# Second FFN up-projection, rounds 3 to 11: seven half-token products in place of eight block products

## The chip, the cores and the metric

The kernel runs on one core of a Trainium2 chip. The metric is the device time of one execution in microseconds. Everything, weights included, is float32; the inputs lie in DRAM.

## The reference, cut to what matters

Two transformer blocks run one after the other over 512 tokens of width 1024. The change touches only the up-projection of the second block's feed-forward part and what hangs on it:

```
h = rms_norm_2(x, ffn_norm_g[l]) * (1 + scale_f) + shift_f
u, v = jnp.split(h @ w_up[l], 2, axis=-1)          # w_up: 1024 x 5632
u = causal_depthwise_conv(u, conv_w[l], conv_b[l])  # width 3 over the tokens
x = x + gate_f * ((jax.nn.silu(u) * v) @ w_down[l])
return rms_norm_2(x, final_g)
```

## The kernel before, in words

**Layout.** Features lie on the 128 partitions, tokens on the free axis: `h` is eight slices of 128 features by 512 tokens. A *tile* `s` is 128 output features. Tiles 156 to 199 (`S_UP2` to `S_DOWN2`) are the second up-projection, tiles 200 to 223 the down-projection behind it. A tile is eight slices `k` deep.

**Float32 by three products.** Every operand is split in a high part (rounded to the matmul's format) and a low part (the rest). `split_product` (L2281 to L2285) issues three matmuls for each slice: high weight by high `h` (L2283), high weight by low `h` (L2284), low weight by high `h` (L2285). A full tile is 8 x 3 = 24 matmuls of 512 columns. Before it, ScalarE (ACT) writes `w_hi` from the landed weights `raw` (L1251 in this stage, L920 elsewhere), and GpSimd (POOL) writes `w_lo = raw - w_hi` (function `lo`, L814 to L821; the instruction has line L820). There are four `w_hi`/`w_lo` buffers and two `raw` buffers; a `raw` buffer holds the two tiles of a *unit*. `w_hi` of tile s waits for tile s-4 to be done, a load waits for the `w_lo` of the tiles that held its buffer.

**A round** is four tiles: two tiles of `u` (t = 0, 1) and the two tiles of `v` for the same features. 11 rounds cover 2816 features. For each t, ACT takes `u` out of PSUM with the middle tap and the bias (L1258), VectorE (DVE) adds the two other taps of the convolution (L1936, L1939), ACT applies silu (L1262), DVE multiplies with the `v` tile out of PSUM (L1930), ACT writes `g_hi` (L1265) and DVE `g_lo = product - g_hi` (L1955). The product stands in `uv`. Each engine walks this list in its own program order, as loops (`ffn_act`, `ffn_dve`, `ffn_pe`); the order between engines is by semaphores alone. `freed["dve"]` counts tiles whose PSUM bank DVE has released: TensorE (PE) waits for it before it starts a tile in the same bank (tile s in bank s % 4 here).

**Ahead of it** the first round is run in halves of 256 tokens because `h` arrives in pieces (`half_tile`, `two_halves`; their matmuls also have the lines L2283 to L2285); DVE and ACT work there on the norm. `xT` holds the residual and is next needed by the down-projection (`last_residual`, L2208).

Of the kernel before, what the change touches and what calls it, by code (L numbers as in the profile page):

```python
# [37 lines left out]
LEVELS = [1, 2, 4, 8, 16, 32, 64]  # L38

# [47 lines left out]
def value_of_step(u):  # L87

    s = step_tile(u - 1)
    return VALUE_TILES.index(s) if u and u % 2 == 0 and s in VALUE_TILES else None  # L90

# [67 lines left out]
def build(nc, a, out):  # L159
# [5 lines left out]
    with ctx:  # L165
# [118 lines left out]
        uv = hn  # L284
        assert max(top1, ada_at + 9216) <= end
# [30 lines left out]
        ps = [nc.alloc_psum_tensor(f"ps{i}", [P, 512], F32) for i in range(8)]  # L316
# [59 lines left out]
        values_turned, values_copied = sem("values_turned"), sem("values_copied")  # L376
        act_chain, dve_chain, pool_chain = sem("act_chain"), sem("dve_chain"), sem("pool_chain")
# [32 lines left out]
        for n in range(S_END // 2):  # L410
# [69 lines left out]
        HALF = T // 2  # L480
# [231 lines left out]
        def _(sp):  # L712
# [85 lines left out]
        def _(pool):  # L798
# [15 lines left out]
            def lo(s, slot=None, count=None):  # L814

                pool.wait_ge(hi_done, s + 1 if count is None else count)
# [3 lines left out]
                pool.tensor_tensor(w_lo[slot % 4][:, 0:nk, :], part[:, :, slot % 2 * P:(slot % 2 + 1) * P],  # L820
                                   w_hi[slot % 4][:, 0:nk, :].bitcast(F32), ALU.subtract).then_inc(lo_done, 1)  # L821
# [77 lines left out]
        def _(act):  # L899
# [7 lines left out]
            def hi(s):  # L907
# [8 lines left out]
                if s >= 4:  # L916
# [3 lines left out]
                act.activation(w_hi[s % 4][:, 0:nk, :], part[:, :, s % 2 * P:(s % 2 + 1) * P],  # L920
# [516 lines left out]
            ffn_act(S_UP2, 1)  # L1437
# [38 lines left out]
        def _(dve):  # L1476
# [742 lines left out]
            ffn_dve(S_UP2, 1)  # L2219
# [60 lines left out]
        def _(pe):  # L2280
# [6 lines left out]
            def tile(s, x, xl, k0=0, first=True, last=True, part=(0, None), ready=None, signal=True):  # L2287
# [567 lines left out]
            ffn_pe(S_UP2, 2)  # L2855
            for n in range(22):
# [5 lines left out]
                down_part(S_DOWN2, n, parts(g_lo_done, FT + 4) if n in (0, 2, 4) else None)  # L2862

            def last_half(q, at=None, between=None):
# [3 lines left out]
                if half == 0:  # L2868
                    pe.wait_ge(lo_done, s + 1)
# [61 lines left out]
```

## Time and profile before

| | |
|---|---|
| median of 3 runs | 1354.01 us (1353.15 to 1357.63) |
| profiled execution: span of its one core | 1350.1 us |
| what lies around the span: median less span | 3.9 us |
| PE busy | 1333.5 us, 99% |
| TensorE clock granted, mean | 0.999 |
| the 36 tiles that change, first matmul to first matmul of tile 200 | 1024.00 to 1219.84 us |

The profiled execution is listed by its span; no time of its own beside it was shown, so the difference to the median stands for what lies around it. Times in rows are microseconds from the start of the span. A matmul's duration in a row contains its way through the array; the rate of a stream is read from the distance between starts.

### The profile page before, as it was taken

How to read it: one execution, taken by the hardware profiler on the slowest of the kernel's cores; microseconds unless marked ns; L12 is line 12 of the kernel's file. 1: busy time of each engine (PE TensorE's matmuls, PEld its weight loads, DVE VectorE, ACT ScalarE, POOL GpSimd, SP SyncE). 2: the span in 40 equal slices, each digit the busy share in tenths (PEclk: the TensorE clock that was granted, in tenths of full speed). 3: DMA queues.
4: the chain of work that ended last, by engine and by line, in shares of the span. 5: the costliest groups of instructions: out<-in, count | busy, mean ns of one | idle time of the engine just before them, and what ended most of it. 6: DMA issues, size and time to landing. Idle time of an engine off the chain costs nothing.

```text
span 1350.1 us, 21809 instructions
## 1 busy us (share of the span) xinstructions
PE 1333.5 (99%) x8014; PEld 1125.5 (83%) x8014; DVE 802.3 (59%) x1626; ACT 618.4 (46%) x1064; POOL 619.3 (46%) x334
## 2 busy tenths in 40 slices
PE   8999999999999999999999998999999999999998
PEld 7878888888998888888889976788998888888887
DVE  5898875456778676767897968714652323221222
ACT  7237566464354545453223535675453434432222
POOL 7545232126364444444544479623354444444441
PEclk9999999999999999999999999999999999999999
DMA  7931121115535444445663232122132222233221
GB/s 218 228 99 47 49 63 49 32 35 171 169 109 160 150 152 146 145 130 164 210 196 122 78 94 65 33 63 63 64 124 93 93 93 93 94 99 104 86 86 63
DMA packets 188315, 146.22 MB, mean 108 GB/s; under 512 B 21561, under 2 KB 186659, under 8 KB 188240
## 3 DMA queue, kind: packets, MB, share of 16 engines
q1 hardware_dynamic: 186528, 144.59, 34.9%
q8 instruction: 50, 0.82, 0.3%
q10 hardware_dynamic: 1200, 0.36, 0.1%
q0 software_dynamic: 512, 0.25, 0.1%
q14 instruction: 25, 0.20, 0.0%
HBM read 143.08 MB, written 2.10 MB: 108 GB/s over the span
## 4 chain that ended last, share of the span: by engine, by line
PE 91%; POOL 4%; DVE 2%; issue 1%; ACT 1%; DMA 0%; DVEq 0%; POOLq 0%; ACTq 0%
PE ps L2283 27%; PE ps L2285 27%; PE ps L2284 27%; POOL w_lo L820 2%; PE ps L2477 2%; PE ps L2533 1%; PE ps L2562 1%; POOL hg L656 1%; PE ps L2762 1%; DVE qd L2077 1%; DVE hf L2085 1%; POOL kd_odd L652 0%; PE ps L2735 0%; PE ps L2367 0%; PE ps L2806 0%
## 5 line engine op out<-in xcount | busy, mean ns | idle before, releaser
L820 POOL TENSOR_TENSOR w_lo<-raw,w_hi 128x1024 fp32r<-128x1024 f32 (+2 forms) x224 | 518.5, 2318 | 666.5 <-ACT w_hi L920 401.6
L2283 PE MATMUL ps<-h_hi,w_hi 128*128 128x512 f32 (+1 forms) x1336 | 497.2, 372 | 0.0
L2284 PE MATMUL ps<-h_lo,w_hi 128*128 128x512 f32 (+1 forms) x1336 | 493.3, 369 | 0.0
L2285 PE MATMUL ps<-h_hi,w_lo 128*128 128x512 f32 (+1 forms) x1336 | 493.0, 369 | 0.0
L2283 PEld LDWEIGHTS ps<-h_hi,w_hi 128*128 128x128 f32 x1336 | 251.8, 188 | 46.0 <-issue 4.7
L2285 PEld LDWEIGHTS ps<-h_hi,w_lo 128*128 128x128 f32 x1336 | 251.8, 188 | 42.8
L2284 PEld LDWEIGHTS ps<-h_lo,w_hi 128*128 128x128 f32 x1336 | 251.9, 189 | 40.7
L920 ACT ACTIVATE w_hi<-raw 128x1024 fp32r<-128x1024 f32 (+2 forms) x136 | 133.5, 984 | 215.3 <-PE ps L2285 194.5
L1251 ACT ACTIVATE w_hi<-raw 128x1024 fp32r<-128x1024 f32 x88 | 93.3, 1060 | 211.8 <-PE ps L2285 211.8
L2283 PE MATMUL ps<-g_hi,w_hi 128*128 128x512 f32 (+1 forms) x394 | 144.9, 368 | 0.0
L2285 PE MATMUL ps<-g_hi,w_lo 128*128 128x512 f32 (+1 forms) x394 | 144.4, 366 | 0.0
L2284 PE MATMUL ps<-g_lo,w_hi 128*128 128x512 f32 (+1 forms) x394 | 144.3, 366 | 0.0
L1887 DVE SCALAR_TENSOR_TENSOR ps<-ada,cond,ps 128x128 f32<-128x128 f32 x336 | 119.6, 356 | 12.0
L2283 PEld LDWEIGHTS ps<-g_hi,w_hi 128*128 128x128 f32 x394 | 74.3, 189 | 12.2
L2284 PEld LDWEIGHTS ps<-g_lo,w_hi 128*128 128x128 f32 x394 | 74.3, 189 | 12.1
L2285 PEld LDWEIGHTS ps<-g_hi,w_lo 128*128 128x128 f32 x394 | 74.3, 189 | 12.0
L1936 DVE SCALAR_TENSOR_TENSOR sq<-ps,small,sq 128x511 f32<-128x511 f32 x44 | 33.0, 750 | 78.1 <-ACT sq L1258 74.8
L2208 DVE SCALAR_TENSOR_TENSOR xT<-ps,small,xT 128x256 f32<-128x256 f32 (+1 forms) x22 | 13.3, 604 | 106.1 <-PE ps L2285 106.1
L1655 DVE SCALAR_TENSOR_TENSOR ps<-z,small,ps 128x512 f32<-128x512 f32 x106 | 70.4, 754 | 0.0
L1930 DVE TENSOR_TENSOR hn<-ps,sq 128x512 f32<-128x512 f32 x22 | 15.2, 691 | 85.9 <-ACT sq L1262 85.9
L1122 ACT ACTIVATE sc<-sc,stat 128x128 f32<-128x128 f32 (+3 forms) x64 | 35.5, 557 | 26.7 <-DVE stat L1668 26.5
L1806 DVE COPY pT<-ps 128x128 f32<-128x128 f32 (+3 forms) x32 | 15.7, 490 | 48.1 <-PE ps L2533 27.0
(373 smaller groups left out, 1703.1 us busy)
## 6 DMA issues: line engine op xcount, KB each, us to landing
ada<-in_ada_w SPq DMA_DIRECT2D x48, 512.0 KB, 3.8
raw<-in_ffn_w_up SPq DMA_DIRECT2D x22, 1024.0 KB, 4.9
raw<-in_w_up SPq DMA_DIRECT2D x22, 1024.0 KB, 4.9
raw<-in_w_in SPq DMA_DIRECT2D x21, 1024.0 KB, 5.1
raw<-in_ffn_w_down SPq DMA_DIRECT2D x8, 896.0 KB, 5.9
raw<-in_w_down SPq DMA_DIRECT2D x8, 896.0 KB, 4.6
raw<-in_w_in SPq DMA_DIRECT2D x16, 256.0 KB, 3.7
raw<-in_w_out SPq DMA_DIRECT2D x4, 1024.0 KB, 5.2
```

The source lines that it names most:

```text
L820: pool.tensor_tensor(w_lo[slot % 4][:, 0:nk, :], part[:, :, slot % 2 * P:(slot % 2 + 1) * P], w_hi[slot % 4][:, 0:nk, :].bitcast(F32), ALU ...
L920: act.activation(w_hi[s % 4][:, 0:nk, :], part[:, :, s % 2 * P:(s % 2 + 1) * P], ACT.Copy).then_inc(hi_done, 1)
L1122: act.activation(x, x, ACT.Exp, scale=-1.0, bias=stat[:, 2 * (j % 2) + g:2 * (j % 2) + g + 1], accum_out=stat[:, 4 + 2 * (j % 2) + g:5 + 2 ...
L1251: act.activation(w_hi[s % 4][:, :, :], part[:, :, s % 2 * P:(s % 2 + 1) * P], ACT.Copy).then_inc(hi_done, 1)
L1655: ins = dve.scalar_tensor_tensor(out=out, in0=src, scalar=w, in1=was, op0=ALU.mult, op1=ALU.add)
L1806: dve.tensor_copy(pT[:, m % 2, 1, 0:L2], ps[7][:, 0:L2]).then_inc(pw_copied, 1)
L1887: dve.scalar_tensor_tensor(out=acc, in0=src, scalar=c, in1=acc, op0=ALU.mult, op1=ALU.add).then_inc(ada_scaled, 1)
L1936: dve.scalar_tensor_tensor(out=u[:, t, 1:T], in0=src[:, 0:T - 1], scalar=col(wname, m + wide), in1=u[:, t, 1:T], op0=ALU.mult, op1=ALU.add ...
L2283: pe.matmul(out_ap, w, x, start=first, stop=False, **kw)
L2284: pe.matmul(out_ap, w, xl, start=False, stop=False, **kw)
L2285: return pe.matmul(out_ap, wl, x, start=False, stop=last, **kw)
L2477: ins = pe.matmul(ps[4 + g][:, 0:L], queries[i][g][part][:, t * P:(t + 1) * P], keys[b][g][:, 0:L], start=part == 0, stop=part == 1)
```

## The change

Rounds 1 and 2 (counted from 1) stay plain tiles, unrolled. The other nine rounds, 36 tiles, become 18 *pairs* p = 0 to 17. A pair is what was one unit: 256 output features by 512 tokens, 1024 deep. It is taken as a two-by-two block product: weight blocks of 512 deep by 128 features, `h` blocks of 512 deep by 256 tokens. Seven products of sums of blocks, each 4 slices deep, 3 matmuls to a slice, 256 columns wide (12 matmuls), take the place of eight. Pairs with even p are `u` tiles, with odd p the `v` tiles of the same round.

- **Sums of `h`** once: T1 to T4, 128 x 1024 elements each. DVE: three adds for T1, two for T2, two for T4 (`t_add`); POOL: three for T3 (`third_sum`). ACT writes their high parts (`t_part_hi`), DVE their low parts (`t_part_lo`). Their room is that of `xT`, so `xT` is stored to DRAM (`x_kept`, 2 MB, two DMAs) and loaded back at the end of the stage. T4 goes over the second-token-half of `h`'s first four slices, after the last plain tile.
- **Sums of weights**, per pair: four adds or subtracts of 128 x 512 by DVE, `w_add(p, 5)`, `(p, 7)`, `(p, 6)`, `(p, 3)`; both operands in SBUF, partly in place in `raw`. Each of the seven products then needs its own `w_hi` (ACT, 128 x 512) and `w_lo` (POOL, 128 x 512): `product_hi`, `product_lo`. The four buffers are used as eight halves.
- **PSUM.** Four banks to a pair. Product 1 gives a value that ACT copies (`copy_one`) as the seed of another region; product 5 is copied to SBUF (`copy_five`); DVE writes two sums in PSUM (`seed_c12`, `make_c22`) on which later products go on adding.
- **Order.** `PRODUCTS` lists the products: 1, 5 of pair 0, then for each p: 6, 2, [1 of p+1], 7, 3, [5 of p+1], 4. PE, ACT and POOL follow it. `g_prod` is a new buffer for the products of `u` and `v`.
- **Loads.** A pair's unit comes as two DMAs of 512 KB; the second waits for the `w_lo` of product 4 of pair p-2, the first for its four sums and the `w_lo` of product 7.

The core of the diff:

```diff
+PLAIN = 2
+PAIR_TILE = S_UP2 + 4 * PLAIN
+NPAIR = (S_DOWN2 - PAIR_TILE) // 2
+PRODUCTS = [(0, 1), (0, 5)]
+for _p in range(NPAIR):
+    PRODUCTS += [(_p, 6), (_p, 2)] + [(_p + 1, 1)] * (_p + 1 < NPAIR) + [(_p, 7), (_p, 3)] \
+        + [(_p + 1, 5)] * (_p + 1 < NPAIR) + [(_p, 4)]
...
@@ SyncE
+                if p < 2:
+                    sp.wait_ge(lo_done, splits(2 * n - 3))
+                else:
+                    sp.wait_ge(w_summed, ONCE + 4 * (p - 2) + 4)
+                    sp.wait_ge(lo_done, product_splits(p - 2, 7))
+                dst, src = k_half(a["w_up_2"][0], (m % 2) * FFN + (m // 2) * 256, n, 0)
+                sp.dma_start(dst, src).then_inc(raw_top[n % 2], 16)
+                unit(n)
...
@@ GpSimd
+            for s in range(S_UP2 + 4, PAIR_TILE):
+                lo(s)
+            third_sum()
+            for p, j in PRODUCTS:
+                product_lo(p, j)
...
@@ ScalarE, product_hi(q)
+                if q < 8:
+                    act.wait_ge(tile_done, PAIR_TILE - 3 + q // 2)
+                else:
+                    after_product(act, *PRODUCTS[q - 8])
...
@@ VectorE
+            def w_add(p, j):
+                if j == 5:
+                    dve.wait_ge(raw_top[u % 2], LANDED + 16 * (p // 2 + 1))
+                    dve.wait_ge(raw_in[u % 2], RAW_COUNT[u])
...
+                    ins = dve.tensor_tensor(w_of(p, 5), w_block(p, 1, 0), w_block(p, 1, 1), ALU.add)
...
+                else:
+                    dve.wait_ge(w_summed, ONCE + 4 * p + 3)
+                    dve.wait_ge(lo_done, product_splits(p, 2))
+                    ins = dve.tensor_tensor(w_of(p, 3), w_block(p, 0, 1), w_of(p, 6), ALU.subtract)
...
+            for r in range(PLAIN - 1):
+                for t in range(2):
+                    taps2(r, t)
+                if r == PLAIN - 2:
+                    t_add(0, hi_of(B12), hi_of(B11), ALU.subtract)
+                    t_add(0, t_sum[0], lo_of(B12), ALU.add)
+                    t_add(0, t_sum[0], lo_of(B11), ALU.subtract, True)
+                for t in range(2):
+                    gated_up(r, t)
...
+            t_add(1, hi_of(B22), t_sum[0], ALU.subtract)
+            t_add(1, t_sum[1], lo_of(B22), ALU.add, True)
+            t_part_lo(0)
+            g_low(r - 1, 0)
+            g_low(r - 1, 1)
+            taps2(r, 0)
+            w_add(0, 5)
+            dve.wait_ge(t_summed, ONCE + 2)
+            taps2(r, 1)
+            w_add(0, 7)
+            w_add(0, 6)
+            gated_up(r, 0)
+            w_add(0, 3)
+            w_add(1, 5)
+            w_add(1, 7)
+            gated_up(r, 1)
+            t_add(3, hi_of(B21), t_sum[1], ALU.subtract)
+            t_add(3, t_sum[3], lo_of(B21), ALU.add, True)
+            t_part_lo(1)
+            t_part_lo(2)
+            g_low(r, 0)
+            g_low(r, 1)
+            w_add(1, 6)
+            t_part_lo(3)
+            for p in range(NPAIR):
+                r, kind = PLAIN + p // 2, p % 2
+                last = PLAIN + (p - 1) // 2
+                if kind:
+                    taps2(last, 1)
+                elif p:
+                    gated_up(last, 1)
+                seed_c12(p)
+                if p and not kind:
+                    g_low(last, 0)
+                    g_low(last, 1)
+                if p + 1 < NPAIR:
+                    w_add(p + 1, 3)
+                make_c22(p)
+                if p + 2 < NPAIR:
+                    w_add(p + 2, 5)
+                    w_add(p + 2, 7)
+                if kind:
+                    gated_up(r, 0)
+                else:
+                    taps2(r, 0)
+                if p + 2 < NPAIR:
+                    w_add(p + 2, 6)
...
@@ TensorE, product(p, j)
+                pe.wait_ge(lo_done, product_splits(p, j))
+                if j == 1:
+                    pe.wait_ge(freed["dve"], FREED[PAIR_TILE + 2 * (p - 2) if p > 1 else PAIR_TILE - 4][1])
+                elif j == 5:
+                    pe.wait_ge(freed["dve"], FREED[PAIR_TILE + 2 * p - 3 if p > 1 else PAIR_TILE - 1][1])
...
+                elif j == 6:
+                    pe.wait_ge(one_copied, ONCE + p + 1)
+                elif j == 7:
+                    pe.wait_ge(c12_seeded, ONCE + p + 1)
+                elif j == 4:
+                    pe.wait_ge(c22_made, ONCE + p + 1)
+                for k in range(4):
+                    ins = split_product(out, w_hi[w][:, ks.start + k, :], w_lo[w][:, ks.start + k, :], x[:, k, :], xl[:, k, :],
+                                        j in (1, 5) and k == 0, k == 3, skip_group_check=True)
```

For product 5 of pair 0 the wait on `freed["dve"]` is for tile 163, which `gated_up(1, 1)` releases (here r counts from 0).

## Rows read from the trace of the kernel before

**Rows 1.** The page: busy time by engine, and the 40 slices of TensorE and its clock.

```profile
PE 1333.5 (99%) x8014; PEld 1125.5 (83%) x8014; DVE 802.3 (59%) x1626; ACT 618.4 (46%) x1064; POOL 619.3 (46%) x334
...
PEclk9999999999999999999999999999999999999999
```

**Rows 2.** Windows: us; busy (count) of PE, PEld, DVE, ACT, POOL; clock; DMA share; GB/s.

```profile
1002.20:1024.00 21.80, 21.80 (x99) 18.04 (x97) 7.31 (x8) 9.37 (x12) 11.95 (x6) 1.00 0.43 145
1024.00:1219.80 195.80, 195.80 (x865) 162.22 (x864) 56.87 (x72) 84.28 (x108) 86.26 (x36) 1.00 0.29 95
```

**Rows 3.** Timeline of TensorE: 28 starts of 256 columns; first matmuls of tiles 164, 200.

```profile
985.83 0.28 PE L2285 MATMUL ps<-h_hi,w_lo 128*128 128x256 f32 x1
...
989.07 0.28 PE L2285 MATMUL ps<-h_hi,w_lo 128*128 128x256 f32 x1
...
1024.00 0.39 PE L2283 MATMUL ps<-h_hi,w_hi 128*128 128x512 f32 x1
...
1219.84 0.39 PE L2283 MATMUL ps<-g_hi,w_hi 128*128 128x512 f32 x1
```

**Rows 4.** Groups by line and shape, 244 to 312 us: 128x512 parts on POOL and ACT.

```profile
L820 POOL TENSOR_TENSOR w_lo<-raw,w_hi 128x512 fp32r<-128x512 f32 x12 | 17.4, 1447 | 47.5 <-ACT w_hi L920 47.5
L920 ACT ACTIVATE w_hi<-raw 128x512 fp32r<-128x512 f32 x12 | 7.6, 629 | 10.4 <-PE ps L2285 10.2
```

**Rows 5.** Timeline of POOL and DVE, 300 to 312 us: 128x512 parts of both.

```profile
302.93 0.69 DVE L1850 TENSOR_TENSOR cv_lo<-acc,cv_hi 128x512 fp32r<-128x512 f32 x1
...
303.02 1.75 POOL L820 TENSOR_TENSOR w_lo<-raw,w_hi 128x512 fp32r<-128x512 f32 x1 [0.98 <-ACT w_hi L920]
...
311.18 1.30 POOL L820 TENSOR_TENSOR w_lo<-raw,w_hi 128x512 fp32r<-128x512 f32 x1 [0.98 <-ACT w_hi L920]
```

**Rows 6.** Timeline of DVE and POOL, 821 to 829 us: 128x1024 operations of both.

```profile
821.10 1.23 DVE L2085 TENSOR_TENSOR hf<-hf 128x1024 f32<-128x1024 f32 x1 [1.41 <-POOL hg L656]
822.36 3.27 DVE L2077 TENSOR_TENSOR qd<-hq,hf 128x1024 f32<-128x1024 f32 x1
...
821.14 3.40 POOL L820 TENSOR_TENSOR w_lo<-raw,w_hi 128x1024 fp32r<-128x1024 f32 x1
824.50 3.34 POOL L652 TENSOR_TENSOR kd_odd<-hk,hg 128x1024 f32<-128x1024 f32 x1
```

**Rows 7.** Timeline of POOL and DVE about one `g_lo` of the stage, then without POOL.

```profile
1047.09 2.40 POOL L820 TENSOR_TENSOR w_lo<-raw,w_hi 128x1024 fp32r<-128x1024 f32 x1 [3.04 <-ACT w_hi L1251]
...
1048.71 1.34 DVE L1955 TENSOR_TENSOR g_lo<-hn,g_hi 128x512 f32 x1 [0.36 <-ACT g_hi L1265]
...
408.79 1.29 DVE L1955 TENSOR_TENSOR g_lo<-hn,g_hi 128x512 f32 x2 [0.32 <-ACT g_hi L1265]
```

**Rows 8.** Groups by line and shape, 1002 to 1219 us.

```profile
L1258 ACT ACTIVATE sq<-ps,small 128x512 f32<-128x512 f32 x20 | 15.2, 759 | 0.0
...
L1930 DVE TENSOR_TENSOR hn<-ps,sq 128x512 f32<-128x512 f32 x21 | 14.5, 691 | 81.1 <-ACT sq L1262 81.1
```

**Rows 9.** Timeline of POOL and DVE in the first round of the stage.

```profile
997.42 9.52 POOL L820 TENSOR_TENSOR w_lo<-raw,w_hi 128x1024 fp32r<-128x1024 f32 x4 [11.18 <-ACT w_hi L1251]
...
1000.67 0.75 DVE L1939 SCALAR_TENSOR_TENSOR sq<-ps,small,sq 128x510 f32<-128x510 f32 x1
```

**Rows 10.** DMA issues by line: KB each, median us from issue to landing.

```profile
raw<-in_w_conv_br SPq DMA_DIRECT2D x4, 512.0 KB, 3.4
...
out<-y_out SPq DMA_DIRECT2D x7, 256.0 KB, 2.0
```

**Rows 11.** Timeline: taps of one tile beside `w_lo`; a PSUM operation on 256 columns.

```profile
1053.27 0.75 DVE L1936 SCALAR_TENSOR_TENSOR sq<-ps,small,sq 128x511 f32<-128x511 f32 x1 [2.62 <-ACT sq L1258]
1054.17 0.75 DVE L1939 SCALAR_TENSOR_TENSOR sq<-ps,small,sq 128x510 f32<-128x510 f32 x1 [0.15 <-DVE sq L1936]
...
1052.54 2.40 POOL L820 TENSOR_TENSOR w_lo<-raw,w_hi 128x1024 fp32r<-128x1024 f32 x1 [3.04 <-ACT w_hi L1251]
...
990.74 0.49 DVE L1502 SCALAR_TENSOR_TENSOR ps<-xT,small,ps 128x256 f32<-128x256 f32 x1
```

More of the change, by code:

```diff
@@ new lines, in _ @@
+            for r in range(PLAIN - 1):
+                for j in range(4):
+                    hi(up_tile(r + 1, 0, j))
+                    if j < 2:
+                        first_tap(r, j)
+                    else:
+                        silu(r, j - 2)
+                if r < PLAIN - 2:
+                    g_high(r, 0)
+                    g_high(r, 1)
+            r = PLAIN - 1
+            t_part_hi(0)
+            g_high(r - 1, 0)
+            g_high(r - 1, 1)
+            product_hi(0)
@@ new lines, in _ @@
+            first_tap(r, 0)
+            t_part_hi(1)
+            product_hi(1)
+            first_tap(r, 1)
+            silu(r, 0)
+            product_hi(2)
+            product_hi(3)
+            silu(r, 1)
+            product_hi(4)
+            t_part_hi(2)
+            product_hi(5)
+            product_hi(6)
+            copy_one(0)
+            product_hi(7)
+            g_high(r, 0)
+            copy_five(0)
+            product_hi(8)
+            g_high(r, 1)
+            t_part_hi(3)
@@ new lines, in _ @@
+            for p in range(NPAIR):
+                r, kind = PLAIN + p // 2, p % 2
+                last = PLAIN + (p - 1) // 2
+                q0 = PRODUCT[p, 6] + 7
+                if p and not kind:
+                    g_high(last, 0)
+                if kind:
+                    first_tap(last, 1)
+                product_hi(q0)
+                if kind:
+                    silu(last, 0)
+                product_hi(q0 + 1)
+                if kind:
+                    silu(last, 1)
+                elif p:
+                    g_high(last, 1)
+                product_hi(q0 + 2)
+                if p + 1 < NPAIR:
+                    copy_one(p + 1)
+                    product_hi(q0 + 3)
+                    product_hi(q0 + 4)
+                if not kind:
+                    first_tap(r, 0)
+                if p + 1 < NPAIR:
+                    product_hi(q0 + 5)
+                    copy_five(p + 1)
+                    product_hi(q0 + 6)
@@ L1438, in _ @@
+            for s in range(S_DOWN2, S_DOWN2 + 4):
+                hi(s)
+            for t in range(2):
+                g_high(FT // 2 - 1, t)
             for n in range(20):
@@ new lines, in gated_up, with g_low @@
+            def gated_up(r, t):
+                n = 2 * r + t
+                dve.wait_ge(silu_done, FT + n + 1)
+                dve.wait_ge(tile_done, up_tile(r, 1, t) + 1)
+                dve.tensor_tensor(g_prod[:, n, :], up_out(r, 1, t), ua[:, t, :], ALU.mult).then_inc(freed["dve"], 1)
+            def g_low(r, t):
+                n = 2 * r + t
+                dve.wait_ge(g_hi_done, FT + n + 1)
+                dve.tensor_tensor(g_lo[:, n, :], g_prod[:, n, :], g_hi[:, n, :].bitcast(F32), ALU.subtract).then_inc(g_lo_done, 1)
@@ L2221, in scaled_out @@
+            r = FT // 2 - 1
+            gated_up(r, 1)
+            for t in range(2):
+                g_low(r, t)
+            dve.wait_ge(x_back, LANDED + 32)
             def scaled_out(k, cols):
@@ L2611, in ffn_pe @@
                             second_sum(b)
+            def ffn_pe(s0, b):
+                first_round(s0, b)
                 with pe.Fori(0, FT // 2 - 1) as i:
```

257 lines of the change are left out of this document (228 added, 29 removed).

## The prediction, on record before the changed kernel ran

> **What bounds the kernel now.** I read the page first: TensorE is busy 99% of the span at full clock [rows 1]. Then the windows of the stage: in the nine rounds that change PE has no idle time at all, POOL works 86 us of 196, DVE 57, ACT 84 [rows 2]. Then the timeline, for the rate of the stream. The 36 tiles, 864 matmuls of 512 columns, take 1219.84 - 1024.00 = 195.84 us, 0.2267 us each; 27 steps of 256-column matmuls take 3.24 us, 0.120 us each [rows 3]. So only matmuls count, as long as the other engines keep up; the reader should see how much room they have now, because the change spends it. Last I looked at how POOL and DVE behave when both work on SBUF, for both get more of exactly that.
>
> **What the change takes off PE.** 18 pairs x 7 products x 12 = 1512 matmuls of 256 columns: 1512 x 0.120 = 181.4 us. Against 195.8 us that is **-14.4 us** (-7.4%, not 12.5%: a half-width matmul costs 53% of a full one). Two extra 256-column matmuls in tile 163: +0.2.
>
> A page would make this more. The Trainium skill (TensorE: Matmul & The Clock Gate, Back-to-back issue gap) gives a warm gap of N/2.4 ns plus about 2.5 ns, by which halving the width costs almost nothing: 864 x 215.8 ns less 1512 x 109.2 ns would be 21.3 us, an estimate by that page. The rows show 226.7 and 120 ns; they decide.
>
> **What a product costs beside PE.** ACT: 7 parts of 0.63 a pair [rows 4], 4.4 us, two PSUM copies below 0.5 each [rows 11], and per pair one tap, silu and high part of at most 0.76 [rows 8]: under 8 of 10.1 us. ACT has cover. Loads: 1 MB a pair as before. A 512 KB load lands in 3.4 us [rows 10], SBUF-to-DRAM is 2.0 us for 256 KB; the 2 MB of `xT`, issued behind the load that follows `w_lo` of tile 159 (near 987), have until 1011: at most 8 x 2.0 = 16 us, so ready near 1003. Hidden; at the end the load back has 25 us until the first residual. Cost nothing; if the store came at 1013 it would add its 2 us.
>
> **DVE and POOL exclude each other.** `w_lo` of 128x512 takes 1.30 us alone [rows 5]. When a DVE operation with both operands in SBUF runs at its start (302.93 to 303.62), it ends at 304.77, which is 1.15 us after DVE. Longer ones alternate strictly: DVE ends at 822.33, POOL 2.21 us later (824.54), the waiting DVE operation 1.09 us later (825.63), POOL again 2.21 us later (827.84) [rows 6]. In the stage itself `g_lo` waits until `w_lo` ends at 1049.49 and ends 0.56 us later, 1.34 us in all; two of them without POOL take 1.29 together [rows 7]. A DVE operation with one operand in PSUM isn't touched: taps take 0.75 in the middle of a `w_lo` [rows 11], the product `ps,sq` 0.69 [rows 8]. So I count, for 128x512: POOL 1.26 back to back (for 128x1024 four take 9.52, 0.03 less each than alone [rows 9]), 1.15 after DVE; DVE 0.56 after POOL. Each two-operand DVE operation then costs a busy POOL 0.56 + 1.15 - 1.26 = 0.45 us.
>
> **Steady state, per round (two pairs).** POOL: 14 x 1.26 = 17.6. DVE's two-operand operations: 8 `w_add`, 2 `g_low`: 10 x 0.45 = 4.5. Sum **22.1 us**, against PE's 20.2. DVE's own list, laid against a POOL that is never idle: a run of two-operand operations advances 1.71 each, one that follows other work waits for the next end of a `w_lo`. Even pair: gated (0.69), seed (0.42), three of them, `make_c22` (0.42), two, taps (1.65), one, ends near 11.6; odd pair: taps, seed, one, `make_c22`, two, gated, one, ends at 19.7. In the odd pair `make_c22` must also wait for product 7 (some 1 us). So DVE needs near 21, POOL 22.1: both over PE's 20.2. Seeds stay on time or about 2 us late in odd pairs, which is the same loss seen on PE. Loss: (22.1 - 20.2) = 1.9 to 2.1 a round (DVE and POOL waiting on each other in turn), 16 pairs with a full list: **+16 us**. Bound below: `w_add` costs POOL nothing, 17.6 < 20.2, no loss. Above: no `w_lo` overlaps with any wait of DVE's, 17.6 + 10 x 0.68 = 24.4 a round, +34. The value is near the middle because rows 6 show the alternation itself.
>
> **Start of the pairs.** On the old clock PE finishes tile 163 at 1024.0 and would start product 7 of pair 0 (the sixth) at 1024.2 + 5 x 1.44 = 1031.4. DVE's list, in order:
> - taps of round 1 end 1001.4 [rows 9]. The three T1 adds (128x1024) alternate with the `w_lo` that POOL has in hand from 997.42: 1002.2 + 3 x 1.09 + 2 x 2.21 = 1009.9. Two gated products: 1011.2 (tile 162 needs them at 1013.1: just in time).
> - POOL's three T3 operations end at 1012.1, 1015.4, 1018.7; between them the T2 adds; `t_part_lo(0)` 1019.8.
> - `w_lo` of the first product, two `g_low` 1022.1, taps 1023.8, `w_add(0,5)` 1024.4, ACT's part and tap, taps 1027.5, two `w_add`, gated 1029.4.
> - `w_add(0,3)` overwrites a block whose `w_lo` (fourth product) must be done: ACT 0.7 and two `w_lo` after `w_add(0,6)` at 1028.8, so 1032.2; it ends 1032.8. Two more `w_add` at 1.71: 1036.2. `gated_up(1,1)`: **1036.9**. Only this releases the bank that product 5, the second, waits for. PE stands from 1025.7: +11.2.
> - Two T4 adds, each behind a `w_lo`: 1038.5, 1040.8; one more `w_lo` 1041.9, `t_part_lo(1)` 1043.0. Product 6 needs it and could have gone at 1038.5: +4.5.
> - `t_part_lo(2)`, two `g_low`, `w_add(1,6)`, `t_part_lo(3)` with POOL idle, seed: 1047.5; product 7 starts 1047.6: +0.3 to 0.5.
> Sum 1047.6 - 1031.4 = **+16.2 us**. Bound below: gated_up ready at 1024.0 and only the T4 sum behind it (0.7 + 2 x 1.1 + 1.1 = 4.0 after 1024, product 6 was due at 1027.1): +1 to +3. Above: every item one `w_lo` later, +25.
>
> **Sum.** -14.4 + 0.2 + 16.0 + 16.2 = +18.0; the last pairs have no `w_add` left and run at PE's pace, already in the 16 pairs. The down-projection's own `w_hi` and `w_lo` fit: POOL is through before PE's last product. Span 1350.1 + 18.0 = 1368.1; with the 3.9 us that lie around it, as in the median before, **1372.0 us**.
>
> **Rivals.**
> - *No exclusion in this pattern (strided adds slip between), start on time.* Steady loss 0, start +1 to +3: 1354.0 - 14.4 + 2 = **1342**. For it: engine totals of 86 and 57 in 196 us look roomy [rows 2]. Against: rows 5 to 7 without exception. It decides only if a `w_add` under a `w_lo` takes 0.68. Chance 0.10.
> - *Half of it:* either the start or the steady loss fails (say DVE finds POOL idle early, or a lead of eight half buffers carries POOL through). -14.4 + 16 = **1356**, 1350 to 1362. For it: eight halves are 11.5 us of lead, but a stalled start doesn't let it grow beyond eight. Chance 0.18.
> - *Lock waits as summed* (my forecast): 1362 to 1384. Chance 0.57.
> - *Another link closes the ring:* the second half load of pair p+2 waits for the `w_lo` of product 4 of pair p, and DVE stands in order before `w_add(p+2,5)` until it lands. From that add: ACT 0.7, two `w_lo` 3.0, load 3.4 to 4, next add 1.2: 8.3 to 9 a pair, under 11. If loads landed 3 us later it would reach 12 a pair: +16 more, **1388**. Or TensorE's clock falls in the stalls: rows 1 show full clock but no stall like 11 us; at half clock (0.24 us a matmul) the three or four products after each early stall cost +5. Chance of over 1384: 0.15.
> The Trainium skill (TensorE: Matmul & The Clock Gate, HAM oscillation) says that idle gaps put the array at half clock; no row here shows such a gap, so its price is only in this last case.
>
> **How the numbers follow.** The likeliest case gives 1372. Its own range is 1362 to 1384. The range of 8 in 10 leaves out the faster rival and the far end: 1355 to 1385. Within 0.3% (4 us: 1350 to 1358) is about what a measurement of this kernel can't tell from no change. Faster: the first rival and a tail of the second, 0.13. Same: most of the second's lower part, 0.10. Slower: 0.77.
>
> **What the profile after would show.** Right: PE idle for some 10 us near 1026, just before the second product's matmuls, released by DVE's product of round 2; DVE adds of 128x512 at mean near 1.1 to 1.3 us where 0.68 is their own; POOL parts of 128x512 with mean 1.45 to 1.55, no idle time; one round (14 products) in 22 us; 256-column steps of 0.120 inside a product; ACT with idle time. Wrong: a POOL mean of 1.3, rounds of 20.2 us, no PE gap. If rounds take over 23 us with POOL idle and DVE waiting for a DMA, the ring of the load is it. If steps inside a product are over 0.12, it is the clock.

## The result, and the profile after

The changed kernel takes **1379.66 us** (median of 4 runs, 1377.55 to 1384.74), the kernel before 1353.63 in the same comparison: ratio 1.0196, 95% interval 1.017 to 1.0222. So it is 26.0 us slower; 1372.0 (1355 to 1385) was forecast. The profiled execution of after took 1381.54, with a span of 1379.8.

The page of the kernel after, busy time by engine and two slice lines (before: [rows 1]):

```profile
PE 1331.7 (97%) x8664; PEld 1151.4 (83%) x8664; DVE 952.4 (69%) x1745; ACT 650.4 (47%) x1174; POOL 739.8 (54%) x427
...
PE   8999999999999999999999998999986989899998
POOL 7545232135445444445543888424377999995441
PEclk9999999999999999999999999999998999999999
```

PE's busy time has hardly moved, but the span has grown by 29.7 us: PE has slices at 8 and 6 in the last third, and POOL stands at 9 in five slices. Windows of the kernel after (columns as in [rows 2]): the last plain tiles, the start of the pairs, the rest of them.

```profile
1006.42:1028.47 22.05, 22.05 (x101) 18.26 (x100) 21.91 (x13) 5.94 (x8) 18.86 (x7) 1.00 0.30 96
1028.47:1056.00 27.53, 12.84 (x92) 12.20 (x91) 20.94 (x21) 12.40 (x22) 15.87 (x12) 0.81 0.13 39
1056.00:1249.52 193.52, 175.62 (x1424) 171.81 (x1422) 163.30 (x168) 107.62 (x201) 178.11 (x116) 1.00 0.31 95
```

The stage of the 36 tiles lasts 1249.52 - 1028.47 = 221.05 us, against 195.84 [rows 3]: +25.2. The first pair also began 4.5 us later than tile 164 had; 0.3 of that arose about the two added matmuls, the rest before 930 us, in code that isn't changed (a granted clock of 0.97 between 800 and 900 us and of 0.83 between 920 and 930, where the profiled execution of before had 1.00). In the twelve variants below the pairs begin anywhere from 1024.2 to 1028.0, so this differs from one execution to the next. After the stage both kernels need 130.3 us. So what the change costs, it costs in the stage. What TensorE waited for in it (PE's waits, kernel after: us in all, times, longest):

```profile
PE ps L2671 <- DVE ps L2535: 14.5, 10, 1.6
PE ps L2671 <- DVE g_prod L2510: 12.1, 1, 12.1
PE ps L2671 <- DVE ps L2539: 4.5, 8, 0.6
PE ps L2671 <- DVE t_lo L2527: 1.6, 1, 1.6
```

L2535 is `seed_c12`, L2539 `make_c22`, L2510 `gated_up`, L2527 `t_part_lo`. The waits of the start, from PE's timeline (two matmuls of product 5, three steps apart, stand between them):

```profile
1042.14 0.55 PE L2671 MATMUL ps<-t_hi,w_hi 128*128 128x256 f32 x1 [12.09 <-DVE g_prod L2510]
...
1043.56 0.41 PE L2671 MATMUL ps<-t_hi,w_hi 128*128 128x256 f32 x1
...
1044.20 0.41 PE L2671 MATMUL ps<-t_hi,w_hi 128*128 128x256 f32 x1
...
1046.62 0.39 PE L2671 MATMUL ps<-t_hi,w_hi 128*128 128x256 f32 x1 [1.58 <-DVE t_lo L2527]
...
1052.23 0.36 PE L2671 MATMUL ps<-t_hi,w_hi 128*128 128x256 f32 x1 [1.02 <-DVE ps L2535]
```

Product 7 of pair 0 starts 23.76 us into the stage, where five products of 1.44 need 7.2: **16.6 us lost at the start**: 15.3 in the three gaps, and 1.3 in 13 slow steps (a step is the time from one matmul's start to the next, slow from 0.15 us on), 11 of them at half clock. From 1036 to 1044 us the granted clock is 0.50, and there a step takes (1044.20 - 1043.56) / 3 = 0.213 us in place of 0.120. For the rounds, groups by line and shape of POOL (1028 to 1250 us) and DVE (1056 to 1220 us):

```profile
L938 POOL TENSOR_TENSOR w_lo<-raw,w_hi 128x512 fp32r<-128x512 f32 x107 | 161.6, 1541 | 20.6 <-ACT w_hi L1590 20.6
...
L2486 DVE TENSOR_TENSOR raw<-raw 128x512 f32<-128x512 f32 x15 | 25.1, 1674 | 0.5
L2494 DVE TENSOR_TENSOR raw<-raw 128x512 f32<-128x512 f32 x14 | 23.8, 1698 | 20.3 <-POOL w_lo L938 20.3
```

The `w_add` of products 7 and 3 take 1.67 and 1.70 us (0.69 beside a short `w_lo`, run 1 below), and DVE stands 20.3 us more ahead of product 3's (L2494). One round on DVE, and on POOL (timelines, kernel after):

```profile
1096.02 0.42 DVE L2535 TENSOR_TENSOR ps<-ps,rstd 128x256 f32<-128x256 f32 x1
1096.35 2.56 DVE L2515 TENSOR_TENSOR g_lo<-g_prod,g_hi 128x512 fp32r<-128x512 f32 x2
1100.17 1.70 DVE L2494 TENSOR_TENSOR raw<-raw 128x512 f32<-128x512 f32 x1 [1.26 <-POOL w_lo L938]
...
1111.67 1.70 DVE L2494 TENSOR_TENSOR raw<-raw 128x512 f32<-128x512 f32 x1 [1.66 <-POOL w_lo L938]
...
1094.90 9.81 POOL L938 TENSOR_TENSOR w_lo<-raw,w_hi 128x512 fp32r<-128x512 f32 x6
...
1109.03 7.21 POOL L938 TENSOR_TENSOR w_lo<-raw,w_hi 128x512 fp32r<-128x512 f32 x5 [1.35 <-ACT w_hi L1590]
```

Six rounds, from the seed at 1086.61 to that at 1224.45, take 137.84 us, **22.97 each**; 14 products of 1.44 are 20.16. Of the 221.05 us, 23.76 are the start and 174.2 the other 121 products; the other 23.1 are lost in the rounds.

### The profile page after: what moved, and what is told of

It reads as the page before. It is cut to its first block, busy times and chain, and to the rows that moved or that the text cites. A ratio compares the mean times of both kernels' runs of the same rounds, so it can differ in the third digit from the quotient of the medians.

```text
span 1379.8 us, 23168 instructions
## 1 busy us (share of the span) xinstructions
PE 1331.7 (97%) x8664; PEld 1151.4 (83%) x8664; DVE 952.4 (69%) x1745; ACT 650.4 (47%) x1174; POOL 739.8 (54%) x427
## 4 chain that ended last, share of the span: by engine, by line
PE 68%; DVE 13%; POOL 11%; issue 4%; DMA 2%; ACT 1%; DVEq 0%; SPq 0%; ACTq 0%; POOLq 0%
PE ps L2671 20%; PE ps L2672 19%; PE ps L2673 19%; POOL w_lo L938 6%; DVE ps L2140 3%; POOL w_lo L932 2%; DMA ada<-in_ada_w 2%; PE ps L2865 2%; PE ps L2921 1%; PE ps L2950 1%; DVE raw L2490 1%; DVE raw L2486 1%; DVE hn L2483 1%; POOL hg L751 1%; DVE sq L2500 1%
## 5 line engine op out<-in xcount | busy, mean ns | idle before, releaser
L932 POOL TENSOR_TENSOR w_lo<-raw,w_hi 128x1024 fp32r<-128x1024 f32 (+2 forms) x188 | 435.7, 2322 | 546.2 <-ACT w_hi L1053 413.2
L2671 PE MATMUL ps<-h_hi,w_hi 128*128 128x512 f32 (+1 forms) x1336 | 469.4, 351 | 4.5 <-DVE ps L2539 4.5
L2672 PE MATMUL ps<-h_lo,w_hi 128*128 128x512 f32 (+1 forms) x1336 | 464.0, 347 | 0.0
L2673 PE MATMUL ps<-h_hi,w_lo 128*128 128x512 f32 (+1 forms) x1336 | 463.4, 347 | 0.0
L2672 PEld LDWEIGHTS ps<-h_lo,w_hi 128*128 128x128 f32 x1336 | 253.9, 190 | 29.7
L1053 ACT ACTIVATE w_hi<-raw 128x1024 fp32r<-128x1024 f32 (+2 forms) x144 | 141.7, 987 | 219.6 <-PE ps L2673 190.5
L938 POOL TENSOR_TENSOR w_lo<-raw,w_hi 128x512 fp32r<-128x512 f32 x108 | 163.9, 1548 | 20.6 <-ACT w_hi L1590 20.6
L1590 ACT ACTIVATE w_hi<-raw 128x512 fp32r<-128x512 f32 x108 | 66.1, 623 | 74.9 <-DVE raw L2494 44.3
L2671 PE MATMUL ps<-t_hi,w_hi 128*128 128x256 f32 x216 | 62.6, 290 | 28.1 <-DVE ps L2535 14.5
L1384 ACT ACTIVATE w_hi<-raw 128x1024 fp32r<-128x1024 f32 x44 | 46.6, 1058 | 90.4 <-PE ps L2673 90.4
L2672 PEld LDWEIGHTS ps<-g_lo,w_hi 128*128 128x128 f32 x394 | 74.3, 188 | 12.1
L2671 PEld LDWEIGHTS ps<-t_hi,w_hi 128*128 128x128 f32 x216 | 41.9, 194 | 30.3 <-issue 27.3
```

Source lines behind the costliest of these rows:

```text
L932: pool.tensor_tensor(w_lo[w_slot(slot)][:, 0:nk, :], part[:, :, slot % 2 * P:(slot % 2 + 1) * P], w_hi[w_slot(slot)][:, 0:nk, :].bitcast(F ...
L938: pool.tensor_tensor(w_lo[w][:, ks, :], w_of(p, j), w_hi[w][:, ks, :].bitcast(F32), ALU.subtract).then_inc(lo_done, 1)
L1053: act.activation(w_hi[w_slot(s)][:, 0:nk, :], part[:, :, s % 2 * P:(s % 2 + 1) * P], ACT.Copy).then_inc(hi_done, 1)
L1384: act.activation(w_hi[s % 4][:, :, :], part[:, :, s % 2 * P:(s % 2 + 1) * P], ACT.Copy).then_inc(hi_done, 1)
L1590: act.activation(w_hi[w][:, ks, :], w_of(p, j), ACT.Copy).then_inc(hi_done, 1)
L2671: pe.matmul(out_ap, w, x, start=first, stop=False, **kw)
```

## The experiments

"Stage" is the time from the first product's first matmul to the first one of tile 200, in the profiled execution. TensorE's own work there is 181.4 us. The last column is its waiting in us in the stage; a slow step behind a wait isn't in it.

| kernel | time, us | ratio to before, 95% | stage | PE's waits |
|---|---|---|---|---|
| before | 1353.6 | | 195.8 | 0 |
| after | 1379.66 | 1.0196 (1.017 to 1.0222) | 221.1 | 32.7 |
| 1: `w_lo` short | 1350.73 | 0.9977 (0.9967 to 0.9988) | 192.7 | 7.2 |
| 2: `w_add` short | 1354.30 | 1.0005 (0.9993 to 1.0016) | 196.3 | 10.9 |
| 3: gate moved | 1379.82 | 1.0199 (1.0182 to 1.0216) | 220.2 | 30.0 |
| 4: sum 3 in another block | 1370.31 | 1.0125 (1.0108 to 1.0142) | 211.5 | 24.7 |
| 5: as 4, start reordered | 1373.32 | 1.0159 (1.0142 to 1.0176) | 213.0 | 24.4 |
| 6: as 4, one block in PSUM | 1356.07 | 1.0029 (1.0018 to 1.0039) | 197.7 | 12.8 |
| 7: as 4, two blocks in PSUM | 1357.73 | 1.0032 (1.0021 to 1.0042) | 198.9 | 12.8 |
| 8: as 7, start reordered | 1358.40 | 1.0044 (1.0031 to 1.0057) | 199.1 | 12.4 |
| 9: as 7, banks swapped | 1352.16 | 0.9988 (0.9976 to 1.0) | 193.5 | 9.2 |
| 10: as 4, banks swapped | 1365.40 | 1.0079 (1.0062 to 1.0096) | 208.7 | 21.4 |
| 11: as 9, start trimmed | 1353.70 | 0.9997 (0.9982 to 1.0013) | 195.9 | 7.4 |
| 12: as 11, gaps filled | 1352.72 | 0.9998 (0.9986 to 1.001) | 193.4 | 3.7 |

The kernel before ran anew in each comparison, with medians of 1353.2 to 1354.6.

**1 and 2. Take the exclusion away, from either side.**

```diff
-                 pool.tensor_tensor(w_lo[w][:, ks, :], w_of(p, j), w_hi[w][:, ks, :].bitcast(F32), ALU.subtract).then_inc(lo_done, 1)
+                 few = slice(0, 16)
+                 pool.tensor_tensor(w_lo[w][:, ks, few], w_of(p, j)[:, :, few], w_hi[w][:, ks, few].bitcast(F32),
+                                    ALU.subtract).then_inc(lo_done, 1)
```

> Edit to the changed kernel: each of POOL's 126 w_lo operations of the pairs works on 16 of the 128 columns of its part (64 elements in place of 512), so most of the low parts of these weights are left out. Nothing else changes; POOL should take about 0.3 us each in place of 1.55. Theory (DVE and POOL exclude each other): the DVE adds of 128x512 fall from means of 1.4 to 1.7 us to about 0.7, the rounds from 22.97 us to PE's 20.2, and the start of the pairs loses about 8 lock waits (16.6 us of stall becomes 8 to 10): 1379.7 - 23 - 7 = about 1350. Rival A (DVE's list is too long by itself, no exclusion): the DVE adds keep their means, rounds stay over 22, about 1378. Rival B (ring through the load of the second half unit): two w_lo less in a ring of 8 to 9 us a pair, loads unchanged; rounds near 22, 1370 to 1378.

> Edit to the changed kernel: each of DVE's 72 w_add operations works on 16 of 128 columns of its block (64 elements), so most of the weight sums are left out. POOL, ACT, PE and the DMAs are as in the changed kernel. Theory (exclusion): POOL's w_lo mean falls from 1.55 to 1.3 to 1.35 us, a round of POOL is 14 x 1.26 + 2 x 0.45 + 8 x 0.15 = 19.7, under PE's 20.2, so rounds take 20.2; the start loses some 6 adds with their waits (-6 us): about 1351. Rival B (ring through the load): the loads and the w_lo stay, rounds stay at 22 or more, 1370 to 1378. Rival C (POOL alone is too slow): w_lo mean stays at 1.55, rounds stay at 21.7 or more.

The first is the edit shown, the second does the same to the four `w_add`; each leaves out most of the numbers that the shortened operations should write. Windows of 1056 to 1200 us of the two kernels, in that order:

```profile
1056.00:1200.00 144.00, 144.00 (x1203) 144.00 (x1202) 87.50 (x143) 94.21 (x171) 40.39 (x100) 1.00 0.34 103
```

```profile
1056.00:1200.00 144.00, 144.00 (x1202) 144.00 (x1201) 111.14 (x143) 95.47 (x174) 133.59 (x101) 1.00 0.34 107
```

PE has no idle time in either: rounds of 20.16 us. With `w_lo` short the unchanged adds of product 7 fall from 1674 to 694 ns; with `w_add` short the unchanged `w_lo` fall from 1541 to 1362. So the loss of the rounds needs both engines: each side alone takes it away, with ACT's work and the loads as they were. Both edits also shorten a list; that the place of the operands decides, and not the length of the lists, is shown by runs 6 and 7. The second kernel stays 3 us above the 1351 that I expected: its rounds are as forecast, its start still waits 10.9 us. Groups of DVE in the second kernel (1056 to 1220 us) show what of an operation is wait:

```profile
L2498 DVE TENSOR_TENSOR raw<-raw 128x64 f32<-128x64 f32 x16 | 20.3, 1272 | 11.1 <-POOL w_lo L938 11.1
```

An eighth of the elements still takes 1.27 us, as long as a whole `w_lo` of POOL. The sums of products 5 and 6 (128x64 too) take 0.68 and 0.67 here.

**3. Only the gate.**

```diff
+            gated_up(r, 1)
             w_add(0, 3)
             w_add(1, 5)
             w_add(1, 7)
-            gated_up(r, 1)
```

> Edit to the changed kernel: in DVE's order gated_up(1,1), which releases the bank for the second product, comes right behind gated_up(1,0), ahead of w_add(0,3), w_add(1,5) and w_add(1,7). Theory (the start is one serial list of DVE, with lock waits): the gap before product 5 shrinks from 12.1 to about 4 us, but product 6 waits for t_part_lo(1), whose place in the list has not moved, so the gap before product 6 grows from 1.6 to about 9.5; total the same within 2 us, 1378 to 1381. Rival: the gap before product 5 is a loss of its own and what follows has slack; then 8 us are gained, about 1372.

The wait for `g_prod` fell from 12.1 to 5.5 us, the one for `t_lo` rose from 1.6 to 8.5: 14.0 in place of 13.7, and the time is that of after. In either order product 6 waits for the sum of the queue.

**4. Break the ring of DVE, ACT and POOL.** In after, sum 3 overwrites the block of product 2 and so waits for its `w_lo`; here it overwrites the block of product 6, whose `w_lo` is one earlier. The ring is this: the sum waits for a `w_lo` of POOL, ACT's next high part for a sum of DVE, and POOL's next `w_lo` for that high part.

```diff
-            return {1: w_block(p, 0, 0), 2: w_block(p, 0, 1), 3: w_block(p, 0, 1), 4: w_block(p, 1, 1),
+            return {1: w_block(p, 0, 0), 2: w_block(p, 0, 1), 3: w_block(p, 0, 0), 4: w_block(p, 1, 1),
...
-                    dve.wait_ge(lo_done, product_splits(p, 2))
+                    dve.wait_ge(lo_done, product_splits(p, 6))
```

The load that refills this block now waits for the `w_lo` of product 3 in place of that of product 7 (a changed line that isn't shown).

> Edit to the changed kernel: w_add(p,3) writes over the block that held the sum for product 6 and waits for the w_lo of product 6 in place of product 2, which comes one w_lo later; the load of the first half unit waits for the w_lo of product 3 in place of 7. Same work. Theory (the rounds of 22.97 us are a ring of DVE and POOL waiting on each other: DVE waits 1.3 to 1.65 us at w_add(p,3) for w_lo, POOL 1.35 us once a round for ACT and w_add(p,6)): the waits at w_add(p,3) nearly vanish, POOL's gap vanishes, rounds fall to POOL's own 14 x 1.26 + 10 x 0.45 = 22.1 and the total by 6 to 7 us, to about 1373. Rival (this wait has slack, the ring is DVE's list with its lock waits alone): rounds stay at 22.9 to 23.0, 1378 to 1380.

The window of six rounds in this kernel, between two seeds:

```profile
1082.42:1214.64 132.22, 122.41 (x1008) 121.36 (x1008) 117.52 (x122) 76.64 (x145) 132.22 (x85) 1.00 0.31 97
```

POOL is busy for all of the 132.22 us, 22.04 a round: this is the floor of 14 x 1.26 + 10 x 0.45 = 22.1 that the prediction had added up. The 0.93 us a round above it in after were the ring. The loss of all rounds falls from 23.1 to 14.0 us, and the kernel by 9.3, more than the 6 to 7 that I expected: 8 x 0.93 = 7.4, the rest lies ahead of these six rounds (PE's wait of 1.6 us at 1064 in after is nearly gone).

**5. The start in another order**, on top of 4: the short work first.

> The kernel with the sum of product 3 over the block of product 6, and besides VectorE's and ScalarE's lists ahead of the pairs in another order: gated_up(1, 1), the two adds of T21 and the splits of T12 and T22 come before w_add(0, 3) and pair 1's sums, and copy_one(0) and copy_five(0) before the high parts of product 6 of pair 1. Theory: of the 16.6 us that the start of the pairs lost in the changed kernel about 6 were VectorE's queue (product 5 of pair 0 waited for gated_up(1, 1) behind w_add(0, 3), (1, 5) and (1, 7)) and the rest the splits on GpSimd; with the short work first, product 7 of pair 0 begins about 6 us earlier, and the rounds stay at 22.05 us: 1364 (1361 to 1367). Rival: the order of VectorE's list only shifts the wait, as when gated_up(1, 1) alone was moved: 1370 (1368 to 1372).

Not six us faster but 3.0 slower in the medians, and 1.5 in the stage of the profiled executions. PE's waits of this kernel:

```profile
PE ps L2673 <- DVE ps L2535: 11.9, 9, 1.7
PE ps L2673 <- DVE g_prod L2510: 5.6, 1, 5.6
PE ps L2673 <- DVE ps L2539: 3.6, 1, 3.6
PE ps L2673 <- DVE t_lo L2527: 3.3, 1, 3.3
```

The first gate is 5.2 us shorter (10.8 in run 4), `t_lo` takes 1.3 of it back and a new one, `make_c22(0)`, 3.6: it stands in DVE's queue behind `w_add(1, 3)`, which waits for a `w_lo` that has itself become late. So the waits are the same in sum (24.4 and 24.7), and product 7 of pair 0, 3.9 us earlier, gains nothing. The 1.5 us are as much as the slow steps of the start grew: 44 of them in place of 28, 4.4 us in place of 2.9. My theory of six us had looked at the gates and not at the list behind them.

**6 to 8. One operand in PSUM.** In [rows 8, 11] DVE operations with an operand in PSUM weren't touched. In each pair two weight blocks are read by three of the four sums. On top of 4, ACT copies the blocks, from pair 2 on, into a PSUM bank that is idle then.

```diff
+            def stage(p, second=0):
...
+                act.activation(stage_at(p), w_block(p, 0 if second else 1, 0), ACT.Copy).then_inc(staged, 1)
...
-                    ins = dve.tensor_tensor(w_of(p, 5), w_block(p, 1, 0), w_block(p, 1, 1), ALU.add)
+                    ins = dve.tensor_tensor(w_of(p, 5), stage_at(p) if p >= 2 else w_block(p, 1, 0), w_block(p, 1, 1), ALU.add)
```

> The kernel with the sum of product 3 over the block of product 6, and besides, from pair 2 on, ScalarE copies the weight block that the sums of products 5 and 7 share into a PSUM bank that is idle then, and the two sums read it there. Theory (two-operand operations of VectorE and GpSimd that both read SBUF alone exclude each other; one operand in PSUM frees both): of 10 such VectorE operations in two pairs 6 are left, GpSimd's floor goes from 14 x 1.26 + 10 x 0.45 = 22.1 to 14 x 1.26 + 6 x 0.45 = 20.3 us a round, just above TensorE's 20.16, so about 1.75 us a round less over 8 rounds: 1356 (1354 to 1360). Rival: the exclusion holds whatever the operands' memory, so rounds stay at 22.05: 1370, or more where ScalarE's added 0.6 us a pair is on the path.

> As the kernel with one block in PSUM, and the other block too (copied by ScalarE over the first when the sum of product 7 has read it), so that the sums of products 5, 7 and 6 each have one operand in PSUM and only four VectorE operations in two pairs read SBUF alone. Theory: GpSimd's floor is 14 x 1.26 + 4 x 0.45 = 19.4 us a round, under TensorE's 20.16; rounds at 20.16 us, 1.9 less than 22.05 over 8 rounds: 1355 (1353 to 1358), the same time as before the change, since the start still loses its 16 us. Rival: the second copy comes late (it waits for the sum of product 7) and holds the sum of product 6 up: rounds above 20.5 us, 1358 to 1366.

> Both: the two blocks in PSUM and the reordered start. If the start's order is worth 6 us and the rounds are TensorE's: 1349 (1346 to 1352), faster than the kernel before the change (1353.6). If only one of the two holds: 1355 to 1364.

Groups of the kernel with one block (1056 to 1200 us) and, below, its window and that of the kernel with two:

```profile
L2501 DVE TENSOR_TENSOR raw<-raw,ps 128x512 f32<-128x512 f32 x14 | 9.6, 687 | 0.5
L2498 DVE TENSOR_TENSOR hn<-ps,raw 128x512 f32<-128x512 f32 x14 | 9.6, 683 | 2.1 <-issue 1.8 <-DMA raw<-in_w_up 0.2
...
1056.00:1200.00 144.00, 144.00 (x1202) 144.00 (x1201) 119.79 (x143) 99.82 (x185) 144.00 (x101) 1.00 0.34 107
```

```profile
1056.00:1200.00 144.00, 144.00 (x1202) 144.00 (x1202) 110.93 (x144) 108.40 (x202) 139.31 (x101) 1.00 0.34 107
```

The same sums take 0.69 us beside a POOL that is never idle, where they took 1.67 and 1.44; the rounds are TensorE's 20.16. The Trainium skill (SBUF — State Buffer, SBUF: two separate sides) says that VectorE locks the port that it shares with GpSimd when both its inputs are in SBUF, and the trace agrees: with one of them in PSUM the wait is gone. With one block POOL is still full (no idle time), with two it has 3% to spare, which brought nothing more (1357.7 against 1356.1). With one block the kernel takes 14 us less than run 4, and the arithmetic is that of after. The reordered start again gave nothing (1358.4).

**9 and 10. Another start.** The even pairs use the upper four PSUM banks and the odd ones the lower (`PAIR_SET = lambda p: 4 * ((p + 1) % 2)`), so that pair 0 waits for no bank of the last plain round; `t_part_lo(1)` and `(2)` come earlier, `make_c22(0)` before `w_add(1, 3)`, and ACT's list follows. What each of these moves is worth by itself isn't shown.

> The kernel with both weight blocks in PSUM, and the start of the pairs built anew: the even pairs use the upper four PSUM banks and the odd ones the lower four, so that pair 0's first products wait for no read of the last plain round's tiles; the splits of T12 and T22 come ahead of gated_up(1, 1) and w_add(0, 3), their high parts as early on ScalarE, and make_c22(0) ahead of w_add(1, 3). What the two earlier variants still waited for at the start was 10.8 + 2.0 us, or 5.5 + 3.6 + 3.3 us: two different gates for about the same 12.5 us. Theory: with the PSUM gate gone and the splits early, all gates but a remnant of 1 to 3 us go, 10 us less than 1357.7: 1348 (1344 to 1351), below the 1353.4 of the kernel before the change. Rival: the work of VectorE and ScalarE behind the last plain tile is itself the limit, and a third gate gives the 12 us back: 1355 to 1359.

> The same new start, without the weight blocks in PSUM (product 3's sum over the block of product 6, rounds at 22.05 us). Theory: the start saves 10 us of 1370.3, unless GpSimd, which sets these rounds, is already behind when the first round begins: then its work, and not TensorE's late start, sets the end, and the saving is smaller, as when the start was reordered before (1373). With GpSimd idle for 3 to 4 us three times in the start of the reordered variant, I take 5 to 10 us less: 1363 (1359 to 1366). Rival: nothing is gained, 1369 to 1373.

5.6 us less with the blocks in PSUM and 4.9 without, half of what I expected of the first and the low end of the second. PE's waits of the first:

```profile
PE ps L2698 <- DVE ps L2560: 2.9, 2, 2.7
PE ps L2698 <- DVE t_lo L2546: 2.8, 1, 2.8
PE ps L2698 <- POOL w_lo L940: 2.3, 2, 1.3
PE ps L2698 <- DVE ps L2556: 1.2, 1, 1.2
```

The one long gate is now five short ones, none over 2.8 us. The kernel is level with the one before, perhaps 0.1% faster (the interval reaches 1.0).

**11 and 12. Trim the start once more, then fill the gaps.** Run 11 moves two `w_add` forward and four `g_low` back in DVE's list, and one `silu` in ACT's; run 12 adds to it 48 matmuls whose results nobody reads.

> The kernel with the weight blocks in PSUM and the banks swapped, and VectorE's list at the start trimmed once more: w_add(0, 5) and w_add(0, 7) come ahead of taps2, and the four g_low of rounds 1 and 2, which only the second FFN's down product reads, go behind make_c22(0). That variant's TensorE still waited 1.3 us for the low part of product 5, 2.8 for the split of T12, 1.0 for a low part, 2.7 for make_c22(0) (behind two g_low of 3.5 us) and 1.2 for a seed: 9 us. Theory: the 1.3 and the 2.7 go, and some of the rest, 4 to 6 us less than 1352.2: 1347.5 (1345 to 1350), faster than the kernel before the change by about 0.5%. Rival: the g_low that are put later hold up the third sum of pair 1 or 2 and a later seed: 1351 to 1354.

> The kernel with the trimmed start, and 48 matmuls of 256 columns more (20 ahead of product 6 of pair 0, 14 each ahead of product 1 of pair 2 and product 7 of pair 1), whose results nobody reads, written to PSUM columns that are unused then: TensorE computes where it stood waiting 2.7, 1.9 and 2.0 us. Nothing of the other engines changes. In the kernel without them the granted clock was 0.64, 0.78 and 0.50 behind these gaps, and 62 of the steps about there took 0.24 us and not 0.12: 6.1 us. Theory: the clock is a term of its own that comes behind TensorE's gaps, it stays at 1.00 with the gaps filled, and all 6 us come back at most, 3 at least, since 5.8 us of fillers can overshoot gaps of 6.6 us a little: 1349 (1347 to 1351), faster than the kernel before the change by 0.3 to 0.5%. Rival: the clock doesn't follow the gaps, or the gap at product 3 of pair 0 (0.8 us) is enough: 1353 to 1356.

Run 11 has less waiting than run 9 (7.4 against 9.2 us) and a longer stage. Windows of its clock, then those of run 12:

```profile
1048.00:1052.00 4.00, 2.09 (x11) 2.00 (x11) 3.86 (x6) 4.00 (x9) 4.00 (x4) 0.78 0.05 12
1052.00:1056.00 4.00, 2.04 (x10) 1.78 (x10) 3.29 (x5) 2.10 (x5) 4.00 (x4) 0.50 0.53 167
1056.00:1060.00 4.00, 4.00 (x21) 4.00 (x21) 2.63 (x4) 1.35 (x3) 4.00 (x4) 0.50 0.25 87
```

```profile
1052.00:1056.00 4.00, 2.69 (x23) 2.48 (x21) 3.96 (x5) 2.05 (x5) 4.00 (x3) 1.00 0.44 135
1056.00:1060.00 4.00, 3.94 (x33) 3.94 (x34) 3.12 (x5) 3.11 (x7) 4.00 (x4) 1.00 0.42 131
```

In run 11 TensorE waited 1.9 us until 1050.0 and 2.0 us until 1054.7. From 1050.2 on the granted clock is 0.50, that is 1.2 GHz, for some 10 us (0.94 between 1060 and 1064): 21 matmuls in 4 us where run 12 has 33. Of the steps of the start, 63 took over 0.15 us and not 0.12, 6.1 us in all, most of them 0.213; my expectation had 0.24 for them. The Trainium skill (TensorE: Matmul & The Clock Gate, HAM oscillation) says that idle gaps put the array at half clock; the trace agrees at these gaps of 2 us, though run 9 kept 1.00 behind one of 2.7. With the gaps filled it stays at 1.00 through the whole start, and 13 slow steps are left, 1.6 us, first behind a wait or about the start of a product: not every slow step is the clock's. The stage became 2.4 us shorter, not 3 to 6. The slow steps gave back 4.5, but 5.8 us of fillers and 3.7 of waits stand where 7.4 of waits had been, so the fillers overshot by 2.1. Against the kernel before both runs are the same; of the time my theory was wrong, of the clock right.

## Why the prediction was right, and where it was off

- **TensorE's saving, -14.4:** right. In the rounds that nothing holds up, 14 products take 20.16 us, 0.120 a matmul.
- **Exclusion, 0.45 us on POOL for each two-operand DVE operation:** right, and shown from three sides (runs 1 and 2, the floor in run 4, PSUM in 6 and 7). The rule "1.15 after DVE, 0.56 after POOL" gave POOL's time for a part as 22.1 / 14 = 1.58; where POOL is never idle (run 4) it is 132.22 / 84 = 1.57. DVE's side I had too low: adds of 128x512 at a mean of 1.1 to 1.3 us were to be seen, and the four measure 1.39, 1.44, 1.67 and 1.70.
- **Steady loss, +16.0:** the term that was mis-sized; it was 23.1. I took 22.1 a round, or a little more, "DVE and POOL waiting on each other in turn". It was 22.97: POOL's floor of 22.1 holds only if POOL is never idle, but sum 3, which waits for `w_lo` of product 2, comes so late, and with it the sums behind it in DVE's list, that ACT and then POOL have no next part for 1.35 us once a round: in the six rounds of after POOL is busy for 129.74 us, 21.6 a round, and stands for 1.35 in each. Run 4 takes this link away and gets 22.04 a round, the forecast, and 14.0 us in all. A detail of the rule was wrong besides: a DVE operation that is released by the end of a `w_lo` loses to POOL's next one and takes 1.70, a whole `w_lo` more, where I had let `w_add(0,3)` go ahead with 0.6. It does so in run 4 too, so that it costs the rounds something by itself isn't shown.
- **Start, +16.2:** 16.6. Its parts came in the forecast order, 12.1 for `g_prod` (11.2), 1.6 for `t_lo` (4.5) and 1.0 for the seed (0.5): 14.7 where 16.2 was forecast, and the rest are slow steps (1.3), which I had left out of the sum, and 0.2 us at each gap in which TensorE sets in again. That the sum is met to 0.4 us is in part luck. The third experiment shows that the split between the first two means nothing.
- **What lies around the span, +3.9:** 1.7 in the profiled execution of after (1381.54 - 1379.8). The difference of a median to one quick execution's span had held 2 us of something else. In that execution, 9.5 us over the forecast, the terms are +7.1 in the rounds, +0.4 at the start, -2.2 here, and +4.3 that arose ahead of the pairs, which no forecast had.
- **The ring of the load, and the clock in the stalls (over 1384, 0.15):** the 512 KB loads landed in 3.5 us and no DVE wait named them. The clock did fall (0.50 from 1036 to 1044 us), but cost some 1.2 us and not 5: TensorE had matmuls for only 11 steps of that time, and a step took 0.213 us and not the 0.24 of the forecast.
- **No exclusion, 1342 (0.10):** what that rival describes is run 1: 1350.7. It too would have been too low, since a wait of 6.5 us at the start and the clock behind it stay.

So the seven products save 14.4 us of TensorE, and ask in each round for 17.6 us of `w_lo` where POOL had 86.26 / 9 = 9.6 [rows 2], and for eight sums beside it: the rounds lose 23 us on the exclusion and its ring, the start 17. With one or two blocks in PSUM the rounds lose nothing; the start still costs 12 us (stage 193.5 less 181.4) in the best version, and the balance is about zero. Whether a start without gaps can be had, which would be worth these 12 us, stays open.

## What to carry to other kernels

When a change moves work from TensorE to VectorE and GpSimd, add up their operations that read SBUF with two operands on both engines together, not engine by engine; where that sum comes near TensorE's, put one operand of the hot VectorE operations in PSUM. Follow each add that works in place back to the read that frees its block: such a link gives the busiest engine idle time that no sum of durations shows. At the start of a software pipeline don't remove a gate by itself, but count the list behind it, and allow for half-clock time behind TensorE's gaps too (1.2 to 5.0 us in the kernels here with gaps left open).

## What the runs showed of the hardware that I had not expected

- In run 11 gaps of TensorE of only 1.9 and 2.0 us went with 10 us at half clock, while run 9 had gaps of 2.7 and 1.2 us in the same place and kept 1.00 there: in all, 1.7 us of slow steps in run 9, 6.1 in run 11. Less waiting doesn't always make a shorter stage.
- Half clock doesn't double the time of these matmuls: a step of 256 columns takes 0.120 us at a granted clock of 1.00 and 0.213 at 0.50, 1.8 times as long.
- A VectorE add of 128x64 beside a busy GpSimd can take 1.22 to 1.27 us (the sums of products 7 and 3 in run 2), almost twice what one of 128x512 takes without it (0.69): the time is the wait for GpSimd's operation to end. The smaller operation gives little of that back, but it holds GpSimd up less (`w_lo` 1362 ns against 1541).
